# Feed-forward seams written out tile by tile, x1 norms taken a phase earlier, and block 0's residual additions on VectorE

## What is computed

```python
def rms_normalize(x, eps):
    xf = x.astype(jnp.float32)
    return xf * lax.rsqrt(jnp.mean(xf * xf, axis=-1, keepdims=True) + eps)
...
    mix = jnp.concatenate([ret_out, diff_out], axis=-1) @ w_out
    x = x + rmsnorm(mix, norm_mix_post)

    u = rmsnorm(x, norm_ffn_pre) @ w_up
    f = jnp.square(jax.nn.relu(u)) @ w_down
    x = x + rmsnorm(f, norm_ffn_post)
```

## Time and profile before

| | us |
|---|---|
| median of 3 runs | 3156.98 |
| lowest, highest | 3156.43, 3160.06 |
| the profiled execution | 3157.81 |
| its span | 3156.0 |

### The profile page before, as it was taken

One profiled execution on the slowest core, in us unless ns is written; L12 is line 12 of the kernel. 1 busy time (PEld: TensorE's weight loads), 2 busy tenths in 40 slices (PEclk: granted clock), 3 DMA queues, 4 the chain that ended last, 5 costly groups with the idle time before them and its releaser, 6 DMA issues.

```text
span 3156.0 us, 39293 instructions
## 1 busy us (share of the span) xinstructions
PE 2898.0 (92%) x14977; PEld 2398.6 (76%) x14977; DVE 1515.4 (48%) x2983; ACT 926.9 (29%) x1838; POOL 318.4 (10%) x437
## 2 busy tenths in 40 slices
PE   5999995999968999999589999999968999999997
PEld 4888884778856766766468888888857998998995
DVE  3232333323246777777344444444456445445446
ACT  3222222222125555555331211211142211211212
POOL 0111110111112111111100000000013000000003
PEclk8999997999979999999789999999988999999999
DMA  4111003333332111110221111111124111111112
GB/s 147 32 34 34 34 21 116 111 113 123 117 122 75 64 64 47 52 41 21 107 68 46 54 40 53 40 53 53 40 69 136 51 40 41 53 40 40 53 54 97
DMA packets 105661, 204.64 MB, mean 65 GB/s; under 512 B 11024, under 2 KB 47888, under 8 KB 105552
## 3 DMA queue, kind: packets, MB, share of 16 engines
q1 hardware_dynamic: 103248, 194.79, 18.7%
q0 software_dynamic: 2304, 8.39, 0.8%
HBM read 168.28 MB, written 34.87 MB: 64 GB/s over the span
## 4 chain that ended last, share of the span: by engine, by line
PE 46%; DVE 2%; ACT 1%; DMA 1%; POOL 0%; issue 0%; SPq 0%; POOLq 0%
PE bank L1907 23%; PE bank L1923 22%; DVE ffn_facc L1806 1%; PE bank L120 1%; DVE ffnp_x L113 0%; ACT ffn_hTh L130 0%; DMA ffnp_x<-x_scratch 0%; DVE ffn_facc L1844 0%; POOL ffnp_rstd L108 0%; ACT ffn_relu L96 0%; ACT ffn_relu L1729 0%; DVE ffn_hidl L1829 0%; DMA ffn_raw<-in_w_up_dram 0%; DVE ffn_dnl L1800 0%; DVE ffn_upl L1793 0%
## 5 line engine op out<-in xcount | busy, mean ns | idle before, releaser
L1907 PE MATMUL bank<-ffn_hTh,ffn_uph 128*128 128x352 f32 (+1 forms) x1280 | 452.5, 354 | 23.3 <-DVE ffn_upl L1793 14.2
L1844 DVE TENSOR_TENSOR ffn_facc<-bank,ffn_facc 128x512 f32<-128x512 f32 x510 | 345.1, 689 | 233.4 <-PE bank L1923 233.0
L1907 PE MATMUL bank<-ffn_hTl,ffn_uph 128*128 128x352 f32 (+1 forms) x1280 | 451.5, 353 | 0.0
L1907 PE MATMUL bank<-ffn_hTh,ffn_upl 128*128 128x352 f32 (+1 forms) x1280 | 450.9, 352 | 0.0
L1923 PE MATMUL bank<-ffn_dnh,ffn_hidh 128*128 128x512 f32 x1088 | 427.3, 393 | 6.4 <-DVE ffn_dnl L1800 3.5
L1923 PE MATMUL bank<-ffn_dnh,ffn_hidl 128*128 128x512 f32 x1088 | 425.6, 391 | 0.0
L1923 PE MATMUL bank<-ffn_dnl,ffn_hidh 128*128 128x512 f32 x1088 | 425.5, 391 | 0.0
L1823 DVE SCALAR_TENSOR_TENSOR ffn_relu<-bank,ffn_relu 128x352 f32<-128x352 f32 (+1 forms) x160 | 94.5, 591 | 499.6 <-ACT ffn_relu L1744 499.6
L1907 PEld LDWEIGHTS bank<-ffn_hTh,ffn_uph 128*128 128x128 f32 x1280 | 242.6, 190 | 48.4 <-DVE ffn_upl L1793 14.5
L1907 PEld LDWEIGHTS bank<-ffn_hTl,ffn_uph 128*128 128x128 f32 x1280 | 242.7, 190 | 23.4
L1907 PEld LDWEIGHTS bank<-ffn_hTh,ffn_upl 128*128 128x128 f32 x1280 | 242.7, 190 | 22.7
(11 more groups left out here) (196 smaller groups left out, 4462.3 us busy)
## 6 DMA issues: line engine op xcount, KB each, us to landing
ffn_raw<-in_w_up_dram SPq DMA_DIRECT2D x64, 512.0 KB, 4.4
ffn_raw<-in_w_down_dram SPq DMA_DIRECT2D x64, 512.0 KB, 4.1
ffnp_x<-x_scratch SPq DMA_DIRECT2D x24, 512.0 KB, 4.4
retp_x<-in_x_prompt_dram SPq DMA_DIRECT2D x16, 512.0 KB, 3.6
retw_raw<-in_w_in_dram SPq DMA_DIRECT2D x8, 1024.0 KB, 5.2
dpp_x<-in_x_prompt_dram SPq DMA_DIRECT2D x16, 512.0 KB, 5.1
dp_kst<-in_cache_diff_k_dram SPq DMA_DIRECT2D x32, 256.0 KB, 2.9
mix_xr<-in_x_prompt_dram SPq DMA_DIRECT2D x16, 512.0 KB, 3.3
```

What stands on the lines that cost most here:

```text
L1844: nc.vector.tensor_tensor(out=part, in0=Dn[i % s.rd][:], in1=part, op=ALU.add).then_inc(s_add, 1)
L1907: last = nc.tensor.matmul(U[i % s.ru][:, 0:w], l[:, k, f * P:(f + 1) * P], r[:, k, c:c + w], start=(k == 0 and q == 0), stop=(k == 7 and q ...
```

## The change

**Mix phase.** `meansq_x(j)` on ACT takes the mean square of x1 of tile j from `xr`; at h == 3 it stands ahead of `y_out(t, 0)`, and for the last two tiles at the phase's end. `rstd_x(j)` on POOL makes 1/rms and keeps it in `keep.rstd_x`, one column for a tile, which lives until the feed-forward phase. SP's `residual_rows(j)` waits for the Square, since it overwrites `xr`.

**Feed-forward phase.** The helper `Prep` is no longer used; no Square, copy and power of x1 are left there. Each engine's list at both block starts is written out tile by tile. `norm_x(t)` on DVE uses the kept 1/rms. A tile is transposed into one pair of banks (`TT`, banks 2 and 3), half by half; the first group's units run in banks 0 and 1 in the order of columns (`first_units`), so that a unit needs only the tiles of its columns. PE's list says best where things stand:

```diff
+                    if s.b == 0:
+                        for t in range(4):
+                            x_transpose(t)
+                        first_up(s, 0, range(0, 4))
+                        x_transpose(4)
+                        first_up(s, 0, range(4, 8))
+                        x_transpose(5)
+                        first_up(s, 1, range(0, 4))
+                        x_transpose(6)
+                        first_up(s, 1, range(4, 8))
+                        x_transpose(7)
+                        first_up(s, 2)
+                        first_up(s, 3)
+                        pe.wait_ge(s_pad, 4)
+                    else:
                         pe.wait_ge(s_h, s.u0)
+                        x_transpose(8)
+                        down(shapes[0], G - 1, 1, 0)
+                        x_transpose(9)
+                        down(shapes[0], G - 1, 1, 1)
+                        x_transpose(10)
+                        down(shapes[0], G - 1, 1, 2)
+                        first_up(s, 0, range(0, 4))
+                        x_transpose(11)
+                        first_up(s, 0, range(4, 8))
+                        x_transpose(12)
+                        first_up(s, 1)
+                        x_transpose(13)
+                        down(shapes[0], G - 1, 1, 3)
+                        first_up(s, 2)
+                        x_transpose(14)
+                        first_up(s, 3)
+                        x_transpose(15)
+                        down(shapes[0], G - 1, 1, 4)
+                        x_transpose(16)
+                        down(shapes[0], G - 1, 1, 5)
+                        first_up(s, 4)
+                        first_up(s, 5)
+                        down(shapes[0], G - 1, 1, 6)
+                        down(shapes[0], G - 1, 1, 7)
```

Tiles 8 to 11 are loaded early into the four x buffers and normed by DVE in block 0's last but one group, behind its tiles 1 to 4. `norm_f`, ACT's `meansq_f` and the residual additions of block 0 move from the first `hidden` of block 1 (the mean squares from its start) into its second, and the additions from POOL to DVE (`first_residual`). POOL keeps the stores and loads. The rest of the diff, cut to its core:

```diff
                 def residual_rows(j):
+                    if j:
+                        sp.wait_ge(s_sx, j)
                     sp.dma_start(xr[0:rows(j), :], xv[j - 1] if j else x_s[0]).then_inc(s_x, 16)
...
                     if h == 3:
+                        if t:
+                            meansq_x(t - 1)
                         y_out(t, 0)
...
+                def norm_x(t):
+                    u, m = slots[t], rows(t)
+                    dve.wait_ge(s_x[u], 16 * loads(t))
+                    nc.vector.scalar_tensor_tensor(out=x[u][0:m, :], in0=x[u][0:m, :], scalar=rstd_x[0:m, t:t + 1],
+                                                   in1=gain_x[0:m, :], op0=ALU.mult, op1=ALU.mult).then_inc(s_xn, 1)
...
+                def first_residual(i):
+                    t = b0[i]
+                    dve.wait_ge(s_xe[0][i % 2], 16 * (i // 2 + 1))
+                    dve.wait_ge(s_fn, t + 1)
+                    nc.vector.tensor_tensor(out=facc[:, i, :], in0=facc[:, i, :], in1=xe[i % 2][:],
+                                            op=ALU.add).then_inc(s_y, 1)
...
                             if ended is not None:
-                                for n in range(2 * i - 2, min(2 * i, ended.nb)):
+                                for n in range(max(2 * i - 4, 0), min(2 * i - 2, ended.nb)):
                                     norm_f(ended, n)
+                                for n in range(max(2 * i - 4, 0), min(2 * i - 2, ended.nb)):
+                                    first_residual(n)
...
                                 accumulate(s, g, tile)
+                                if s.b == 0 and near and 1 <= tile <= 4:
+                                    norm_x(7 + tile)
...
+                def x_transpose(t):
+                    pe.wait_ge(s_xn, t + 1)
+                    for b in range(2):
+                        if t:
+                            pe.wait_ge(s_lo, 2 * t - 1 + b)
```

More of the change, by code:

```diff
@@ L1733, in meansq_f, with relu @@
                                          bias=NORM_EPS).then_inc(s_mf, 1)
-                def hidden(s, g, e):
+                def relu(s, g, i, units):
+                    f, c, w = units[i]
                     k0 = s.u0 + g * s.ku
+                    bank = U[i % 2] if units is s.first_units else U[i % s.ru]
+                    act.wait_ge(s_u, k0 + i + 1)
+                    if i >= 2:
+                        act.wait_ge(s_hl, k0 + i - 1)
+                    nc.scalar.activation(rh[i % 2][:, 0:w], bank[:, 0:w], ACT.Relu).then_inc(s_r, 1)
@@ L1758, in _ @@
-                    for i, t in enumerate(s.tiles):
-                        if i + 1 < s.nb:
-                            pre.act_meansq(act, slot(t + 1), loads(t + 1), t + 2)
-                        pre.act_hi(act, t, t + 1, rows(t), i % 2)
-                        if s.b == 0 and i == 1:
-                            up_hi(1, s)
-                        if s.b and i:
-                            meansq_f(shapes[0], i - 1)
-                    hidden(s, 0, 0)
+                    fu = s.first_units
@@ L1898, in up @@
                 def up(s, g):
[L1899 to L1900 removed]
+                    second = isinstance(g, int) and g == 1
+                    pe.wait_ge(s_wlo, 4 * G * s.b + 4 * g)
                     k0 = s.u0 + g * s.ku
[L1902 to L1910 removed]
+                    for i, unit in enumerate(s.units):
+                        pe.wait_ge(s_h, k0 if second and i < s.ru else k0 + i + 1 - s.ru)
+                        up_unit(U[i % s.ru], unit, range(8)).then_inc(s_u, 1)
```

428 lines of the change are left out of this document (280 added, 148 removed).

## The result

The changed kernel takes **3142.18 us** (median; 3140.71 to 3143.8) against 3160.06 for the kernel before (3156.43 to 3163.52), each run five times on one chip: ratio **0.9941**, 95% interval 0.9929 to 0.9954. It is faster, as forecast, but by 0.6% and not by 1.2%: 3142 lies 8 us above the range of 3108 to 3134. The profiled execution spans 3140.8 us, 15.2 less than before; forecast were 36.6.

What follows compares the result with a forecast made beforehand. PE was taken to be bound by its clock and idle seams at phase start and change of block, with no gaps between. Terms -11.6, -27.0 and +2.0 take 3156.98 to 3120 us; range 3108 to 3134 for 8 in 10.

Steps and rivals of the forecast that it cites:

- Term A: Start of the feed-forward phase: no Square, copy and power, up-projection behind four tiles instead of eight; second up-projection 11.6 us earlier.
- Term B: Block 0's last but one group to block 1's second up-projection: tiles and weights overlapped, that up-projection starts 40.3 us earlier.
- Term C: Block 1's first down-projection: PE waits for DVE's norms and additions; 13.3 us given back, change of block nets -27.0.
- Term D: Phase before the feed-forward: ACT's added Square and copy mostly fit its slack; +2 us, bounds 0 and 20.
- rival 2: Block 0's residual additions: GpSimd's powers come late behind DVE and hold it; 9.7 us, 3130 in all; chance 0.14.
- 1 (loads do not bind): Block 1's first down-projection: row loads land in 3.6 us, DVE alone sets the pairs; 5 us less, 3115; chance 0.13.
- 3: Phase before the feed-forward: every insertion on ACT reaches PE; 18 us more, 3138; chance 0.10 together with 5.
- 5: Inserted tiles: each of 12 makes PE wait a whole round, 1.5 us more; 3138; chance 0.10 together with 3.
- 4, a low clock: Phase start and change of block: chopped order keeps PE at the lower level; up to 84 us, half gives 3162; chance 0.04.

Runs made afterwards that it cites:

- b3_flat: Kernel before with only the halves of its hidden tiles 1056 columns apart instead of 1152, no other tile moved: 3175.9 us, ratio 1.0048.
- a2_hid1152: Changed kernel with the hidden tiles' old layout, halves 1152 columns apart instead of 1056: 3128.8 us, ratio 0.9895 to the kernel before.
- d1: a2_hid1152 with block 0's eight residual additions on GpSimd again instead of DVE: 3126.3 us, ratio 0.9887 to the kernel before.
- m1: Kernel before with only the change's mix-phase part added (1/rms of x1 computed but not used): 3165.3 us against 3160.1.
- d2: a2_hid1152 with three buffers instead of two for the x1 rows of block 0's residual additions: 3122.3 us, ratio 0.9879 to the kernel before.
- c2: a2_hid1152 with hidden-tile halves 1024 columns apart in block 0 and 1088 in block 1: 3126.2 us, ratio 0.9887 to the kernel before.
- c1: a2_hid1152 with hT's eight parts 1024 columns apart instead of 1056 in block 0: 3118.9 us, ratio 0.9862 to the kernel before.
- a1: Changed kernel with every tile of the last three phases 32 bytes further: 3142.6 us, ratio 0.9939 to the kernel before.
- b4: Kernel before with every tile of the last three phases 32 bytes further: 3163.0 us, ratio 1.0006.

## Why the prediction was right and wrong

- **The direction, and the mechanism of what is reordered, were right.** First up matmul: forecast 17.3 us earlier behind the phase's start, measured 16.3 (20.85 against 37.18). PE idle ahead of tile 0's down-projection: forecast 2.4 us (2290.8 less 2287.3 and 1.06 for the transposes), measured 2.7. Ahead of tile 9's transposes: forecast 5.2, measured 3.1, because tile 0's down-projection between the two ran at the lower clock (a matmul each 0.43 us, 2292.03 to 2296.29) and so filled 2 us of that wait, which ACT and DVE end anyhow. None ahead of block 1's second up-projection: none. One wait in the first down-projection, released by the copies into facc, with DVE waiting for rows: forecast 14 us, measured 16.3. The forecast of 3120 us stands 22 us off all the same, mostly because the sum had no term for what the new layout costs.
- **The step that failed** is the sentence in "What bounds the kernel now" that these groups "follow one another without a gap, so order can gain nothing there", and the sum that gave them no term. Without a gap they are, before and after, and the statement is true of the order. But the diff also changes the shape of the hidden tiles, which I took for bookkeeping, and their matmuls pay 5 ns each. +14.1 us of the 21.4 by which the sum missed; b3_flat shows it alone (+14), a2_hid1152 without it comes to 3128.8, inside the range. The other 7.3 us are errors of size: 1.9 in term A, 3.5 in the change of block (terms B and C), 1.9 in term D. Why a distance of 4224 bytes costs 5 ns is not known.
- **Term A**, -9.8 for -11.6. The first norm starts 5.94 us behind the phase's start, not 5.4, since the gain's load, issued second, takes 5.54 and lands last; the first up-projection comes another 0.5 later, and the stretch from it to the second one takes 36.3 us for 35.4. These three are small errors of size.
- **Term B**, from the last but one group to the second up-projection, was 63.9 us where 63.5 was worked out: right. After tile 9 the largest gap of PE there is 0.41 us.
- **Term C** is where the 3.5 us of the change of block went. The restart came 43.4 us behind the second up-projection's start, not 41.1. Addition 0 ended 16.5 us behind that start, as worked out (16.6); what failed is the time from it to the last low part, 26.2 us and not 23.8. The term for the landing of the x1 rows was too small: the three loads in the chain took 5.60, 5.33 and 5.91 us and not 4.98, 1.9 us of the 2.4 (DVE waited 7.6 us for rows in all). GpSimd's powers took up to 1.48 us beside DVE and not 0.55, but only one of them stands in the chain, so rival 2 came true in a weak form only. The rest of that down-projection took 23.4 for 22.4, half of it by the 5 ns. That the additions stand on DVE and not on GpSimd has no part in it: d1.
- **Term D** was +2 and is under 2 by the pairs of traces, about 1 by the runs of m1 at equal clock; most of the +3.9 of the ledger is the clock's. The profile of the kernel before that I started from is one of those with the least time lost to it, and the kernel's median in the later series was 3160 to 3162, not 3157.
- **The rivals**: 1 (loads do not bind) fell, d2 shows that they bind for 6 us; 3 and 5 fell; 4, a low clock, did not come in the two seams (0.91 over the change of block for 0.83 before, 0.64 over the start of the phase for 0.55) but decides the length of the phase before. The case that came true was not on the list.

## What to carry to other kernels

Read a diff for what it does to the shapes and distances of matmul operands, not only for what it does to order: a tile made 96 columns narrower cost 14 of the 33 us that the reordering gained, and nothing in the trace of before, where all operands of that stage had the good distance, would show a wait for it. Where one stage's matmuls run a few per cent slower than another's of equal size, compare the distances of their operands: that difference stood in the profile of before (21.82 against 22.26 us for 96 matmuls) and was worth about 8 us. And when seams are tightened, work that was parked behind them becomes the next wait: look for idle slots of the same engine inside the seam before leaving it in one piece.

## What the runs showed of the hardware

- Matmuls of 512 columns followed one another in 226.7 ns with the parts of the weight operand 4096, 4352 or 4608 bytes apart, and in 231.7 with 4224 (changed kernel, a2, c2); for the streaming operand in 226.7 with 4096 and in 232.2 with 4224 (c1, changed kernel). Moving all tiles by 32 bytes made no difference (a1, b4). The granted clock was 1.00 in the groups at 232 ns (changed kernel) and in those at 227 (a2).
- Beside each other, a DVE norm with two SBUF inputs and a GpSimd addition took 3.36 and 2.33 us; alone the norm takes 1.24. Moving the additions between them made no difference that can be told (d1).
- The phase before took 642.9 to 650.7 us in programs whose work there differs by less than 2 us at equal clock, as the granted clock of its middle part was 0.99 or 0.97. A run's mean granted clock told the time of the same kernel to about 2.3 us for each 0.001.
